# Half of the forward output coefficients of the S5 tiles on GpSimd instead of VectorE

## The reference

```
u = x @ w_in                                  # 1024 x 1024, groups of 16 channels
lam_bar = exp(lam * step); b_bar = ((lam_bar - 1) / lam) * b
h[l] = lam_bar * h[l-1] + b_bar @ u[l]        # complex, 64 states a group, forward and backward
y[l] = Re(c @ h[l])                           # both directions added
out = (gelu(y + d*u) gated) @ w_out
```

## Time and profile before

| | us |
|---|---|
| median of 3 executions | 2761.36 (2760.3 to 2762.53) |
| the profiled execution's own time | 2760.96 |
| its span in the trace | 2759.2 |
| TensorE busy | 2560.7 (93%) |
| VectorE busy | 1833.4 (66%) |
| GpSimd busy | 830.0 (30%) |
| ScalarE busy | 812.1 (29%) |

### The profile page before, as it was taken

One profiled execution on the slowest core, in us unless ns is written; L12 is line 12 of the kernel. 1 busy time (PEld: TensorE's weight loads), 2 busy tenths in 40 slices (PEclk: granted clock), 3 DMA queues, 4 the chain that ended last, 5 costly groups with the idle time before them and its releaser, 6 DMA issues. The chain is left out here.

```text
span 2759.2 us, 40511 instructions
## 1 busy us (share of the span) xinstructions
PE 2560.7 (93%) x13124; PEld 2145.8 (78%) x13124; DVE 1833.4 (66%) x3173; ACT 812.1 (29%) x1376; POOL 830.0 (30%) x606
## 2 busy tenths in 40 slices
PE   6787699999999999978999999997899999999996
PEld 5576587878888888866888888886687888888884
DVE  7799617666666666583667666667675666666667
ACT  3223314433333232213222323222133233322220
POOL 2968410433333332412111111110034333323340
PEclk8899899999999999999999999998999999999998
DMA  4333314134443443412010111000413444434341
GB/s 136 89 101 103 96 31 153 46 100 135 129 125 106 127 124 106 145 56 66 24 39 23 38 30 36 25 23 16 152 43 103 116 136 123 120 112 138 107 130 61
DMA packets 388063, 246.16 MB, mean 89 GB/s; under 512 B 23936, under 2 KB 370176, under 8 KB 387072
## 3 DMA queue, kind: packets, MB, share of 16 engines
q1 hardware_dynamic: 387968, 244.92, 29.8%
HBM read 227.10 MB, written 17.76 MB: 89 GB/s over the span
## 5 line engine op out<-in xcount | busy, mean ns | idle before, releaser
L928 DVE TENSOR_TENSOR h<-h,ps 128x512 f32<-128x512 f32 x320 | 219.2, 686 | 150.0 <-PE ps L537 149.7
L2142 POOL TENSOR_TENSOR w_lo<-w_raw_plain,w_hi 128x1024 fp32r<-128x1024 f32 x38 | 93.0, 2455 | 553.0 <-ACT w_hi L62 553.0
L2170 PE MATMUL ps<-aT_hi,w_hi 128*128 128x512 f32 x624 | 250.6, 402 | 3.9 <-DVE hg_q_raw L2431 2.0
L2170 PE MATMUL ps<-aT_hi,w_lo 128*128 128x512 f32 x624 | 245.5, 394 | 0.0
L2170 PE MATMUL ps<-aT_lo,w_hi 128*128 128x512 f32 x624 | 244.2, 391 | 0.0
L1041 POOL TENSOR_TENSOR s5o_w_sets_plain<-s5o_w_sets_plain 128x512 f32<-128x512 f32 x100 | 137.4, 1379 | 221.9 <-DMA s5o_w_sets_plain<-in_ffn_w_in_dram 221.9
L1041 POOL TENSOR_TENSOR hgo_w_sets_plain<-hgo_w_sets_plain 128x512 f32<-128x512 f32 x100 | 136.4, 1369 | 223.6 <-DMA hgo_w_sets_plain<-in_ffn_w_in_dram 223.6
L479 PE MATMUL ps<-aT_hi,s5o_w_sets 128*128 128x512 f32 x640 | 202.9, 393 | 0.0
L479 PE MATMUL ps<-aT_hi,hgo_w_sets 128*128 128x512 f32 x640 | 202.8, 393 | 0.0
L537 PE MATMUL ps<-s5o_w_hi,s5o_hid_hi 128*128 128x512 f32 x352 | 138.6, 394 | 14.1 <-DVE aT_lo L865 13.5
L62 ACT ACTIVATE s5o_w_sets<-s5o_w_sets_plain 128x512 fp32r<-128x512 f32 x152 | 92.7, 627 | 182.9 <-POOL s5o_w_sets_plain L1041 155.6
(11 more groups left out here) (386 smaller groups left out, 6346.7 us busy)
## 6 DMA issues: line engine op xcount, KB each, us to landing
s5o_w_sets_plain<-in_ffn_w_in_dram SPq DMA_DIRECT2D x208, 256.0 KB, 3.3
hgo_w_sets_plain<-in_ffn_w_in_dram SPq DMA_DIRECT2D x208, 256.0 KB, 3.3
w_raw_plain<-in_hg_w_in_dram SPq DMA_DIRECT2D x40, 512.0 KB, 4.0
s5o_w_sets_plain<-in_ffn_w_in_dram SPq DMA_DIRECT2D x96, 128.0 KB, 2.8
hgo_w_sets_plain<-in_ffn_w_in_dram SPq DMA_DIRECT2D x96, 128.0 KB, 2.7
s5o_w_lo_plain<-in_ffn_w_out_dram SPq DMA_DIRECT2D x11, 1024.0 KB, 5.1
hgo_w_lo_plain<-in_ffn_w_out_dram SPq DMA_DIRECT2D x11, 1024.0 KB, 5.1
h<-in_x_dram SPq DMA_DIRECT2D x4, 1024.0 KB, 9.2
```

The lines of the kernel that those rows point to most:

```text
L928: v.tensor_tensor(to, to, ps[:, 4 + m % 4, :], ALU.add).then_inc(S["out_acc"], 1)
L2142: g.tensor_tensor(w_lo[b][:, :, :], w_raw[b][:, :, :], w_hi[b][:, :, :].bitcast(F32), ALU.subtract).then_inc(E[f"w_lo_done{b}"], 1)
L2170: ins = t.matmul(ps[:, half, :], w[b][:, kk, :], x[:, kk, cols], start=(kk == 0 and q == 0), stop=(kk == KT - 1 and q == 2))
```

## The change

For tiles 1 to 7 the first two of the four forward rows of `cl` are made by GpSimd, in memory, ahead of the backward half; VectorE keeps the last two, in the banks as before. `make_cl` takes the rows as an argument. `CLF` falls to 6, since VectorE's set is one group of six instructions, and GpSimd's counter goes up by 12 a tile, so `make_kern` waits for `2 * (n + 1) * CLS`. Tile 0 is as it was.

```diff
-    BAR, BL, CLS, CLF = 6, 12, 6, 12
+    BAR, BL, CLS, CLF = 6, 12, 6, 6
@@
-    def make_cl(e, n, d, sem, base):
+    def make_cl(e, n, d, sem, base, rows_=slice(0, PR)):
         link = Steps(sem, base)
-        c = [bc(c_all[:, d, q, n * PR:(n + 1) * PR, :], 2, [P, PR, L + 1, GRP])
-             for q in range(2)]
-        out = [cl[n % 2][:, q, d * PR:(d + 1) * PR] for q in range(2)]
-        product_steps(link, e, c, powers(n, d, slice(0, PR)), out, gen_t[:, :, :, :], conj=True)
+        c = [bc(c_all[:, d, q, n * PR + rows_.start:n * PR + rows_.stop, :], 2,
+                [P, rows_.stop - rows_.start, L + 1, GRP]) for q in range(2)]
+        out = [cl[n % 2][:, q, d * PR + rows_.start:d * PR + rows_.stop] for q in range(2)]
+        product_steps(link, e, c, powers(n, d, rows_), out, gen_t[:, rows_, :, :], conj=True)
@@ make_cl_in_psum
-        for b in range(2):
-            rows_ = slice(2 * b, 2 * b + 2)
+        for rows_ in (slice(2, 4),):
@@ make_kern
-                t.wait_ge(S["cl"], (n + 2) * CLS)
+                t.wait_ge(S["cl"], 2 * (n + 1) * CLS)
@@ GpSimd
-                make_cl(g, n, 1, S["cl"], (n + 1) * CLS)
+                make_cl(g, n, 0, S["cl"], 2 * n * CLS, slice(0, 2))
+                make_cl(g, n, 1, S["cl"], (2 * n + 1) * CLS)
```

## The result

The changed kernel takes 2783.84 us (median of 6 executions, 2782.87 to 2788.22), the kernel before 2761.95 (2758.34 to 2763.53): a ratio of 1.0085 with a 95% interval of 1.0074 to 1.0095, 21.9 us slower. The forecast was 2785.1, with a range of 2777.5 to 2789.

What follows compares the result with a forecast made beforehand. The S5 tile loop was taken to be bound by a ring through GpSimd's coefficients, with VectorE outside it. 5d - 4.2 = 18.4 us plus 5.3 us of clock made 23.7 us, so 2785.1 us, range 2777.5 to 2789.

Steps and rivals of the forecast that it cites:

- The ring: S5 loop, tiles 3 to 5: input products, ScalarE's weight rounding, GpSimd's low part and backward coefficients, then kern; slack 0.60, 1.51, 0.65 us.
- Five of seven additions on the path: Of GpSimd's added work in tiles 1 to 7, five additions delay the end, cl(2) and cl(7) being covered: 18.4 us.
- the five places named: Turn of tile 2, kern(3), kern(4), kern(5) and turn of tile 7, each forecast to be released by GpSimd.
- VectorE's gain in tiles 3 to 6: VectorE's saved 2.71 us a tile is covered by start_state ahead of the scan, worth 0.1 us a tile on the path.
- d: GpSimd's added time per tile for six instructions on 128x288, from a straight line between two shapes: 4.53 us, good to 0.4.
- Rival D: GpSimd's 288-column instructions cost more than the straight line, 5.3 us a tile, giving 2789 us; chance 0.07.
- The clock: TensorE runs at half clock after new idle gaps: 1.3 us at turn of tile 2, 2.0 each at kern(3) and kern(4); 5.3 us.
- Rival A: GpSimd delays the loop as forecast, but TensorE's clock doesn't fall in the short gaps: 2779.8 us; chance 0.24.
- The waits: TensorE's idle gaps ahead of kern(3), kern(4) and kern(5), forecast at 3.9, 3.1 and 3.9 us.
- The fall at kern(5): Clock loss at kern(5) in tile 5 doesn't count, because GpSimd has already gone on to the chain that is late last.
- 0.75 us of idle time goes: Tile 7: TensorE's idle time ahead of kern(7), right behind VectorE's last coefficient, disappears: gain 0.75 us.
- The sum: Whole kernel: 18.4 us of GpSimd delay plus 5.3 us of clock, 23.7 us slower, 2785.1 us; chance 0.57.

Runs made afterwards that it cites:

- the relief alone: Kernel before, with VectorE making only its last two forward rows in tiles 1 to 7 and nobody making the other two: 2762.10 us, ratio 1.0003.
- the two kernels with fill matmuls: Changed kernel plus eight or fifteen unused 512-column matmuls ahead of kern(3) to kern(5), in TensorE's wait for GpSimd: 2783.41 us with eight, 2781.05 us with fifteen.

## Why the prediction was right

**The ring.** Five of seven additions on the path: shown. Tiles 2 and 7 cost nothing, tiles 3 to 5 cost 15.8 us, the slope is 5.1, and GpSimd is the releaser at the five places named. VectorE's gain in tiles 3 to 6 was put at about nothing, and the relief alone buys nothing measurable.

**d.** Estimated by a straight line at 4.53 us, measured 4.53. Rival D (5.3) is out. The Trainium skill, GPSIMD Engine Reference (3.1, Elementwise), has 1.96 times VectorE's cost for an fp32 add of 2048 columns; these traces have 4.53/2.71 = 1.67 times, and the measurement decides.

**The clock, in the right place and too large.** Put at 5.3 us, it is 4.3 by the traces: 1.3 at the turn of tile 2, as forecast (3.83 us against 2.54), and 1.4 and 1.6 at kern(3) and kern(4) instead of 2.0 each. That term was mis-sized. In the traced execution 0.95 us came back by chance at start_state(2), which took 4.99 instead of 5.94 us. It wasn't owed to the slower turn: behind the same turn of 3.83 us start_state(2) took 6.47 and 6.16 us in the two kernels with fill matmuls. Rival A, no fall of the clock in such short gaps, is wrong in mechanism, as kern(3) took 1.94 us. The waits were forecast at 3.9, 3.1 and 3.9 us and are 3.02, 4.41 and 2.21: kern's start is set by GpSimd, and start_state ahead of it took 6.54, 5.13 and 6.64 us in tiles 3 to 5, where before it had taken 5.06, 6.57 and 5.64. The clock around the gap of tile 3, in windows (columns as above):

```profile
173.00:174.00 1.00, 1.00 (x12) 1.00 (x11) 0.92 (x2) 0.00 (x0) 0.92 (x2) 0.50 0.00 0
174.00:175.00 1.00, 0.77 (x14) 0.53 (x10) 0.19 (x1) 0.00 (x0) 1.00 (x1) 0.97 0.00 0
...
176.00:177.00 1.00, 0.00 (x0) 0.00 (x0) 0.97 (x3) 0.00 (x0) 0.92 (x2) 1.00 0.00 0
177.00:178.00 1.00, 0.22 (x5) 0.20 (x8) 0.96 (x2) 0.00 (x0) 0.92 (x2) 0.73 0.00 0
...
180.00:181.00 1.00, 1.00 (x7) 1.00 (x6) 0.93 (x3) 0.20 (x2) 0.90 (x2) 0.56 0.07 16
181.00:182.00 1.00, 1.00 (x11) 1.00 (x10) 0.97 (x4) 0.00 (x0) 1.00 (x2) 1.00 0.00 0
```

The granted clock had just risen to 2.4 GHz when TensorE ran out of work at 174.8; it fell to 1.2 shortly before work came back at 177.78, and rose at some 180.9. So TensorE worked at half clock for 3.1 us, not for the 5.2 of kern(0), from which the 2.0 was taken. The fall at kern(5) did not count, as the prediction had it: behind it GpSimd has no idle time from 237.46 us, where its low part of the weights starts, to the end of bl(7) at 297.74.

**Tile 7.** The step "0.75 us of idle time goes" was read from kern(7) and missed that turn(7) hung on VectorE. That did no harm, since in the changed kernel bl(7) comes later than the diagonal: 297.74 against 295.23. The 0.75 us did go, but start_state(7) ahead of kern(7) took 6.18 instead of 5.21 us in that execution, so kern(7) is at +22.0, no sooner than turn(7) with +21.8.

**The sum.** Forecast were 23.7 us more than before, and 21.9 came. With the clock term as measured the sum is 18.4+4.3 = 22.7 us; the remaining 0.8 is within the interval of the measurement (20.4 to 26.2 us), and no two large errors cancel in it. That the shifts of the trace lie 0.5 to 2.7 us below the forecast has two more sources in that one execution: it was 0.45 us ahead at kern(0) already (89.99 against 90.44), and the 0.95 us of start_state(2). Over its whole span the traced execution is 27.2 us longer, not 21.9. At the single GpSimd product of line 1110, far behind S5, it is 20.7 us late (1198.64 against 1177.99 us). The other 6.5 come after that, in code that the change doesn't touch, and the granted clock was lower there in that execution. The same stretch of work, before:

```profile
1180.00:1240.00 60.00, 46.55 (x207) 37.83 (x206) 54.83 (x108) 5.33 (x10) 4.21 (x2) 0.89 0.15 62
1240.00:1300.00 60.00, 49.52 (x232) 40.35 (x231) 13.76 (x30) 24.15 (x37) 9.06 (x4) 0.98 0.23 61
```

and after, 20 us later:

```profile
1200.00:1260.00 60.00, 46.55 (x194) 37.57 (x193) 53.44 (x108) 5.33 (x10) 4.85 (x2) 0.83 0.13 53
1260.00:1320.00 60.00, 55.23 (x245) 44.76 (x243) 9.76 (x16) 18.87 (x31) 7.17 (x3) 0.94 0.25 70
```

The medians don't carry it. Why the clock was lower there in that execution is not known.

## What to carry to other kernels

Idle time counts only by its place, and a busy share only by its stretch: GpSimd is 30% busy over the span, but 78% between 120 and 260 us (109.33 of 140 us). Work for such an engine is free where its idle time comes after that work in program order, and costs all of it but the slack, plus the clock, where the idle time comes before. So read the slack just before each consumer (here 0.6, 1.5 and 0.65 us), tile by tile, and count the places where the new work is larger. When an engine's product is late for one consumer, move the consumer behind work that doesn't need it before moving work between engines: that alone gained 8.8 us in the old kernel, and with the states copied earlier 17.2.

## What the runs showed of the hardware

- With eight fill matmuls, idle gaps of 1.80 and 1.76 us (tiles 3 and 4) were followed by half clock: around the first the granted clock was 1.00 from 174 to 180 us, 0.80 in the next microsecond, with TensorE at work again since 179.40, and then 0.50 up to 184. Behind the gap of 1.58 us in tile 5 it stayed at 1.00, as it did behind the gaps of 0.27 us and less. By the Trainium skill, TensorE: Matmul & The Clock Gate (Why this matters for your kernels), idle gaps between bursts bring the slow clock back; the trace agrees. The page has it for longer gaps than these, and here the measurement decides: 1.80 and 1.76 us were enough.
- A fall of the clock costs what runs in it: 1.4 to 1.6 us for the 112 short matmuls of kern, within and across.
- The moment at which the clock rises is not the same from tile to tile or from execution to execution: in tiles 2 to 7 of the changed kernel the 64 matmuls of start_state took between 4.99 us (tile 2) and 6.64 us (tile 5); in tile 3, with 6.54 us, the granted clock was 0.50 up to 174 us, until shortly before their end. A difference of 1 us between two traces can be that alone.
- On GpSimd a straight line between 128 and 576 columns gave the time of three instructions of 288 columns to 0.01 us (2.27).
